# Five two-vector conditioning panels moved from a down GEMM and a mixer GEMM into an up GEMM

## The reference

```python
cond = silu(c)
for l in range(2):                                   # first block
    mod = cond @ w_ada[l] + b_ada[l]                 # 9216 columns, one vector
    y = (silu(h @ w_gate) * (h @ w_up)) @ w_down     # FFN, in{l}0 and out{l}0
    ...                                              # mixer: mix, gate, branch, mixout
    y = (silu(h @ w_gate) * (h @ w_up)) @ w_down     # FFN, in{l}1 and out{l}1
for layer in range(2):                               # second block
    mod_l = silu(c_2) @ mod_w_2[layer] + mod_b_2[layer]      # 6144 columns
    mod_c = silu(c_ctx_2) @ mod_w_2[layer] + mod_b_2[layer]  # the same weights
```

## Time and profile before

| | |
|---|---|
| median of three runs | 2908.57 us (2908.52 to 2911.18) |
| profiled execution: own time | 2913.43 us |
| its span, first to last instruction | 2911.6 us |
| its mean granted clock of TensorE | 0.981 |
| busy: TensorE matmul, VectorE, ScalarE | 2697.7, 1943.9, 1091.0 us |
| out10, mix1, in11, out11 begin near | 876, 957, 1246, 1373 us |

### The profile page before, as it was taken

One profiled execution on the slowest core, in us unless ns is written; L12 is line 12 of the kernel. 1 busy time (PEld: TensorE's weight loads), 2 busy tenths in 40 slices (PEclk: granted clock), 3 DMA queues, 4 the chain that ended last, 5 costly groups with the idle time before them and its releaser, 6 DMA issues.

```text
span 2911.6 us, 48608 instructions
## 1 busy us (share of the span) xinstructions
PE 2697.7 (93%) x18294; PEld 2294.3 (79%) x18294; DVE 1943.9 (67%) x3303; ACT 1091.0 (37%) x1389; POOL 240.3 (8%) x135
## 2 busy tenths in 40 slices
PE   3999999999999989999989969999999889989998
PEld 3998988899998888899868844787644667668887
DVE  6776666777777756666755382677696676664781
ACT  2434432443542434154464551433201644432211
POOL 0000000000000000000022300344200000000000
PEclk9999999999999999999999989999999999999999
DMA  8775735677575553545412201222367221113442
GB/s 308 261 286 200 294 123 191 235 276 288 211 269 225 202 187 118 188 145 204 186 59 82 73 15 44 73 94 94 140 239 278 87 73 59 59 61 128 152 164 74
DMA packets 106384, 469.15 MB, mean 161 GB/s; under 512 B 7052, under 2 KB 57304, under 8 KB 58328
## 3 DMA queue, kind: packets, MB, share of 16 engines
q1 hardware_dynamic: 106200, 466.67, 44.2%
HBM read 465.58 MB, written 1.06 MB: 160 GB/s over the span
## 4 chain that ended last, share of the span: by engine, by line
PE 48%; DVE 24%; DVEq 9%; ACT 6%; DMA 6%; issue 5%; ACTq 1%; SPq 1%; POOLq 0%
PE accs L680 7%; PE accs L695 7%; PE accs L696 7%; PE accs L697 7%; DVE panel_r L86 5%; DVEq L2870 4%; PE accs L832 4%; DMA panel<-w 3%; DVE arena L2847 3%; DVE arena L2151 2%; PE accs L1241 2%; ACT arena L76 2%; PE accs L1242 2%; PE accs L1243 2%; DVE cond_panel L2151 2%
## 5 line engine op out<-in xcount | busy, mean ns | idle before, releaser
L695 PE MATMUL accs<-normed_r,arena_r 128*128 128x256 f32 (+2 forms) x1864 | 585.2, 314 | 17.6 <-DVEq L2196 7.3
L696 PE MATMUL accs<-arena_r 128*128 128x256 f32 x2069 | 584.7, 283 | 0.0
L697 PE MATMUL accs<-normed_r,panel_r 128*128 128x256 f32 (+2 forms) x1872 | 584.3, 312 | 0.0
L86 DVE TENSOR_TENSOR panel_r<-panel,arena_r 128x1024 fp32r<-128x1024 f32 (+1 forms) x295 | 390.1, 1322 | 165.7 <-ACTq L1515 120.4
L1514 ACT ACTIVATE arena_r<-panel 128x1024 fp32r<-128x1024 f32 (+1 forms) x292 | 330.4, 1132 | 385.7 <-DMA panel<-w 143.1
L695 PEld LDWEIGHTS accs<-normed_r,arena_r 128*128 128x128 f32 (+1 forms) x1864 | 350.4, 188 | 55.2 <-issue 12.8
L696 PEld LDWEIGHTS accs<-arena_r 128*128 128x128 f32 x2069 | 389.6, 188 | 1.1 <-issue 0.2
L697 PEld LDWEIGHTS accs<-normed_r,panel_r 128*128 128x128 f32 (+1 forms) x1872 | 350.2, 187 | 23.5 <-issue 0.4
L680 PE MATMUL accs<-normed,panel 128*128 128x256 f32 x1536 | 340.5, 381 | 5.2 <-ACT normed L76 2.4
L2847 DVE SCALAR_TENSOR_TENSOR arena<-accs,vectors,arena 128x189 f32<-128x189 f32 (+2 forms) x704 | 279.4, 428 | 94.9 <-issue 66.1
L680 PEld LDWEIGHTS accs<-normed,panel 128*128 128x128 f32 x1536 | 288.8, 190 | 51.2 <-issue 4.9
(11 more groups left out here) (424 smaller groups left out, 4666.9 us busy)
## 6 DMA issues: line engine op xcount, KB each, us to landing
panel<-w SPq DMA_DIRECT2D x250, 1024.0 KB, 4.9
panel<-w SPq DMA_DIRECT2D x48, 1408.0 KB, 7.9
cond_panel<-wc SPq DMA_DIRECT2D x57, 1024.0 KB, 6.3
normed<-wc SPq DMA_DIRECT2D x43, 1024.0 KB, 6.5
arena<-wc SPq DMA_DIRECT2D x19, 1024.0 KB, 5.4
residual<-xs SPq DMA_DIRECT2D x2, 1024.0 KB, 9.6
residual<-wc SPq DMA_DIRECT2D x1, 1024.0 KB, 13.0
residual<-crows SPq DMA_DIRECT2D x2, 512.0 KB, 8.9
```

What stands on the lines that cost most here:

```text
L86: i = self.eng.tensor_tensor(*a, **k)
L695: pe.matmul(out, hi[:, k, 0:m], src_hi(k), start=clear and k == 0, stop=False, skip_group_check=True)
L696: pe.matmul(out, hi[:, k, 0:m], src_lo(k), start=False, stop=False, skip_group_check=True)
L697: mm = pe.matmul(out, lo[:, k, 0:m], src_hi(k), start=False, stop=last and k == n - 1, skip_group_check=True)
```

## The change

The table gives out10 two paired panels (72, 73) for five, mix1 six (74 to 79) for eight, mixout1 four with new numbers (80 to 83), and in11 five (84 to 88), which it had none of; out11 keeps 89 to 91. In in11 a panel is loaded and weighed only in the body with u = 1 of each group of four panels, five in all: one ahead of the loop, four in it. All five land in one place, the first half of `normed`, and are signalled on a semaphore of their own; the load of one waits until the weighing of the one before is done. The counts that later stages wait for on the two old semaphores are lowered by what no longer lands on them. The bias additions of `cond_take` run behind in11 too, through the line that asks whether a stage is in the table.

```diff
 CARRY = {"head": (0, HEAD), "in00": (8, 11), "out00": (19, 7), "mix0": (26, 10), "branch0": (36, 3), "mixout0": (39, 4),
-         "in01": (43, 11), "out01": (54, 7), "in10": (61, 11), "out10": (72, 5), "mix1": (77, 8), "mixout1": (85, 4), "out11": (89, 3),
+         "in01": (43, 11), "out01": (54, 7), "in10": (61, 11), "out10": (72, 2), "mix1": (74, 6), "mixout1": (80, 4), "in11": (84, 5), "out11": (89, 3),
          "gate2": (92, 4), "pairs": (96, 8), "down0": (104, 16)}
...
-    if phase[:2] == "in":
+    if phase == "in11":
+        units = [(it, 0)] if u == 1 else []
+    elif phase[:2] == "in":
         units = [(it * 2 + u // 2, u // 2)] if u % 2 == 1 else []
...
-                    if not isinstance(i, int) or i + n0 >= 2:
+                    if phase == "in11":
+                        sp.wait_ge(S("cond_done"), i + n0)
+                    elif not isinstance(i, int) or i + n0 >= 2:
                         sp.wait_ge(S("cond_done"), i + (n0 - 1))
...
-                    sp.dma_start(cond_slot(phase, slot), src).then_inc(cond_landed[slot], 16)
+                    sp.dma_start(cond_slot(phase, slot), src).then_inc(S("late_landed") if phase == "in11" else cond_landed[slot], 16)
...
-                    dve.wait_ge(cond_landed[slot], i * 8 + (8 * (n0 - slot) + 16 - 48))
+                    before = 48 if n0 < CARRY["in11"][0] else 96 if slot == 0 else 80
+                    dve.wait_ge(S("late_landed"), i * 16 + 16) if phase == "in11" else \
+                        dve.wait_ge(cond_landed[slot], i * 8 + (8 * (n0 - slot) + 16 - before))
```

## The result

The changed kernel takes **2924.6 us** (median of 5 runs, 2922.57 to 2930.81). The ratio to the kernel before is **1.0046 [1.0034, 1.0057]**, and 1.0038 [1.0025, 1.0050] when it was timed again. (The kernel before had two more runs beside it, and a median of 2908.57 again, 2907.11 to 2911.39; the plain quotient of the medians is 1.0055.) It is slower, as forecast, but by more: 2915.4 had been given, with a range up to 2919.5. The profiled execution took 2924.73 us, with a span of 2922.9 us and a mean granted clock of 0.978.

What follows compares the result with a forecast made beforehand. Out10 loses TensorE time in gaps ended by VectorE, which also bounds mix1's weighings; in11 keeps TensorE busy. Terms -7.4 - 4.2 - 0.9 + 11.6 + 0.5 + 6.8 + 0.4 = +6.8 on 2908.57 give 2915.4 us, range 2907.5 to 2919.5.

Steps and rivals of the forecast that it cites:

- Out10, -7.4: Second layer's first down GEMM: three of five weighings leave, TensorE's four gaps of 6.6 us go; -7.4 us (-7.7 to -6.5).
- Mix1, -4.2 and -0.9: Mix1: last two of eight weighings go with their gaps, -4.2 us; even chance of low clock behind the new last gap, -0.9.
- In11's gaps, +11.6: In11's loop: each of four weighings delays TensorE by 2.9 us, gap and recovery; +11.6 us (+8.8 to +12.6).
- rival C: In11: VectorE's spare time absorbs the weighings and TensorE stays fed; sum -11.6, 2897.0 us; chance 0.07.
- rival D: In11: each weighing is exposed whole and the product with it, 21.4 in place of 11.6; 2925.2 us; chance 0.05.
- E: Rival: out10's gaps are set by landings and stay, so VectorE's relief brings nothing there; +14.2, 2922.8 us; chance 0.03.
- The clock in in11, +6.8: In11's loop: a drop to 1.2 GHz behind each of four new gaps, 1.7 us each; +6.8 us (0 to 6.8).
- Rival B: In11: gaps come as forecast, but the clock holds (2908.6 us) or falls in one or two groups (two: 2912.0); chance 0.24.
- First weighing, +0.5: Ahead of in11's loop: the first weighing falls into a 4.72 us wait for ScalarE; +0.5 us (0 to 1).
- Out11, +0.4: Behind in11, ahead of out11's low parts: two added bias additions on VectorE, 0.41 us; +0.4 us (0 to 0.9).
- The median of the three timed runs is 4.86 below that own time, so 2908.57 + 6.8: Whole kernel: base taken from three runs' median, below the profiled execution's 2913.43 us; with the sum of terms, 2915.4 us.
- That unedited stages stay as they were: Stages outside the edit: no change entered in the sum; ScalarE's copies, POOL's sums and TensorE's instructions taken as unchanged.

Runs made afterwards that it cites:

- The halves: Changed kernel with each of the four weighings in in11's loop cut in two, at u = 1 and u = 2: 2908.36 us, ratio 0.9981 to the kernel before.

## Why the prediction was right or wrong

- **Out10, -7.4: right.** Stretch I gives -7.5; no gap of it is left.
- **Mix1, -4.2 and -0.9: the sum is right against the profile it was made from**, -5.1, but by luck. Where before's low clock is hidden, as in its second profile, II is 284.3, so the two weighings are worth 3.6 and the drop that was paid in the first profile 1.5. Behind the new last gap the clock fell in one of eleven profiles, not in every second one. The term for the clock was a fact of one execution, and it was entered into a sum for the median.
- **In11's gaps, +11.6: right**, 2.67 us where 2.5 to 2.8 was said, 2.93 a group with recovery where 2.9 was said. A reading of averages would have failed: VectorE had 43 us idle, 24.8 were added, and TensorE still idled 10.7. The halves show that rival C lacked only the place, not the time. The measured 2924.6 is within 1 us of rival D's 2925.2, but D's 5.4 us exposed in each group are not there, and neither are the gaps in out10 that E kept.
- **The clock in in11, +6.8: right in kind, a little too large.** Four stretches of low clock in each of four profiles with the 2.67 us gaps; a group takes 27.09 us with one and 25.55 without, so each costs 1.5 beyond gap and recovery, and the four 6.2. The reading of the Trainium skill ("TensorE: Matmul & The Clock Gate", "Part 1: The HAM clock gate") that a stage busy as a whole keeps its clock would have made it 0.0; these rows speak against it: the stage is busy 116.26 of 127 us and the clock fell all the same. Rival B is out: without the drops the sum would have been near 0.
- **First weighing, +0.5: right**, a gap of 0.89 against 0.41. From the start of stretch III to the end of out11's gap the offset between the two traces grows by 18.96 us; less 0.93 for out11's gap that is 18.0 for in11, where the steps gave 18.9. The clock makes most of the difference; a gap of 0.74 us at the start of in11 before, which is gone, makes 0.4.
- **Out11, +0.4: wrong, the term of the sum that was mis-sized most.** It measured +2.5: 0.93 for the gap, from 1.30 to 2.23 us, and 1.5 for the low clock behind it. The bias additions were counted as VectorE's 0.41 us. Moving them brings back 0.32. The gap itself comes from SP's queue, where a conditioning load waits for a weighing ahead of weight panel 3; the panel took 8.51 us from issue to ScalarE's read against 8.02 before. The text looked at SP's queue in in11 and ahead of it, not in out11. And the drop that was priced behind every gap in in11 was not priced behind this one.
- **The step that failed by most is the last one: "The median of the three timed runs is 4.86 below that own time, so 2908.57 + 6.8".** In 90 further runs the kernel before had medians of 2912.9 to 2915.1 and a spread of 2906.6 to 2918.1, so its profiled execution, 2913.43, was a common one, and the three runs, within 3 us of each other, were not. The changed kernel came out at 2924.60 and 2924.63. About 4.7 of the 9.2 us that the forecast missed lie in this base. Why the base was low stays open. Scatter between executions is a poor explanation: beside the changed kernel's first timing the kernel before had the same median of 2908.57 in five runs, none above 2911.39, and only 23 of the 90 later ones are as low as that. If something else made it faster in those first timings, neither its own profiled execution nor the changed kernel shared it.
- **That unedited stages stay as they were** was a term put at nothing without a reason. By the ratios it failed by some 4 us; five places located in the traces make 3.3.
- **Together:** from 2913.3 the same steps give 2920.1; with the edited stretches as profiled, +7.9, they give 2921.2; with the five places 2924.5.
- **The range.** Its upper end, 2919.5, is more than its own terms give: 2915.4 with mix1 keeping its drop (0.9), out10 at its worse bound (0.9) and in11 at 12.6 (1.0) is 2918.2. The measured time lies above either.

## What to carry to other kernels

Vector work that fits a stage on average still has to fit between two due times; halving the piece was worth 16 us here, and moving it by one body 13, at the same work. Price a gap of TensorE as three terms: itself, about 0.26 us of recovery, and possibly low clock behind it, 1.5 us where that was paid in in11. That last term was near certain behind gaps of 2.67 us in in11 and not behind shorter ones elsewhere; ask of it whether another engine's work hides it. And take the base of a forecast from as many executions as can be had, at more than one time: here five runs at 2908.57 and ninety at 2913.3 were of one kernel.

## What was not expected of the hardware

- How often low clock follows a gap of TensorE in in11 and out11, by length: 1.70 us: 0 of 4; 1.87 and 1.91: 1 of 2; 2.22 and 2.23: 5 of 7; 2.67: 15 of 16, with twice the usual length behind one of them. In mix1 it is 5 of 19 at 1.77 to 1.90 us and 2 of 11 at 2.18 to 2.28, so the length alone doesn't tell.
- One low stretch cost 1.5 us in in11's groups (27.09 against 25.55), 1.5 behind out11's gap and 2.0 behind mix1's last gap (282.7 against 280.7), and nothing between mix1's weighings, where VectorE is the bound (280.7 with one such stretch there and with two).
- The same kernel's executions spread over 11.6 us (2906.6 to 2918.1), 0.4%, at equal work.
- A new deal of panels moved idle times of VectorE that have no releaser in stages as far as 1400 us behind out11, the same in eleven programs. One of them lengthened a gap of TensorE by 0.34 us, and in ten of the eleven the clock then fell behind that gap.
